# Expert weights by ranked expert: four fixed experts first, then a pattern of shared and full-width steps

## The reference, cut to what matters

```python
p_group = softmax(hf @ w_group + b_group)            # 4 groups
g_sel = argmax(p_group)
fine = (hf @ w_router + b_router).reshape(N, 4, 8)
top_v, top_i = lax.top_k(fine[g_sel], 2)             # two experts of the group
gate = softmax(top_v) * gate_g
expert = g_sel * 8 + top_i                           # 32 experts, 512 x 2 = 1024 routed rows
# for every expert e, on the rows routed to it:
gt, up = split(x_rows @ w_gu[e], 2)                  # 1024 -> 2 x 256
y = (silu(gt) * up) @ w_down[e]                      # 256 -> 1024
out[token] += gate * y
```

## Time and profile before

| | us |
|---|---|
| median of 3 runs | 2167.5 (2164.75 to 2168.77) |
| the profiled execution | 2168.4 |
| its span, first to last instruction | 2166.6 |
| first expert step starts (PE) | 1872.2 |
| last expert matmul ends | 2144.7 |
| PE busy | 2075.0 (96%) |
| bytes moved | 284.9 MB |

### The profile page before, as it was taken

One profiled execution on the slowest core, in us unless ns is written; L12 is line 12 of the kernel. 1 busy time (PEld: TensorE's weight loads), 2 busy tenths in 40 slices (PEclk: granted clock), 3 DMA queues, 4 the chain that ended last, 5 costly groups with the idle time before them and its releaser, 6 DMA issues.

```text
span 2166.6 us, 31540 instructions
## 1 busy us (share of the span) xinstructions
PE 2075.0 (96%) x13636; PEld 1524.9 (70%) x13636; DVE 1106.3 (51%) x1777; ACT 734.0 (34%) x1130; POOL 161.5 (7%) x140
## 2 busy tenths in 40 slices
PE   8999999999999998999999999999899999898887
PEld 6886688888888785788888887566788848532223
DVE  8886555335436876555335446476633353421114
ACT  6445632212324446532212333244322213311112
POOL 1220000000000320000000020000000001011121
PEclk9999999999999999999999999999999999899999
DMA  5222033322222231122222221312111315699996
GB/s 191 69 84 79 20 122 122 121 102 97 96 97 69 79 103 39 40 97 98 98 97 97 97 79 66 107 40 78 60 61 61 114 63 236 269 417 419 419 416 240
DMA packets 52254, 284.89 MB, mean 131 GB/s; under 512 B 9280, under 2 KB 9536, under 8 KB 22160
## 3 DMA queue, kind: packets, MB, share of 16 engines
q1 hardware_dynamic: 45344, 264.32, 32.9%
q0 software_dynamic: 6192, 17.64, 2.1%
q10 hardware_dynamic: 576, 0.87, 0.1%
HBM read 270.41 MB, written 22.02 MB: 135 GB/s over the span
## 4 chain that ended last, share of the span: by engine, by line
PE 75%; DMA 9%; DVE 9%; ACT 4%; issue 1%; SPq 1%; DVEq 0%; ACTq 0%
PE psum L126 73%; DMA ring_moe<-in_w_dn 8%; DVE A_mix L139 3%; PE psum L129 2%; ACT A_mix L133 1%; DVE WL L139 1%; DVE A_second L139 1%; ACT A_mix L136 1%; ACT WH L133 1%; SPq L171 1%; DMA M<-in_m 1%; DVE A_mix L165 1%; DVE A_second L147 0%; DVE A_mix L147 0%; DVE A_mix L159 0%
## 5 line engine op out<-in xcount | busy, mean ns | idle before, releaser
L139 DVE TENSOR_TENSOR WL<-raw,WH 128x1024 fp32r<-128x1024 f32 x236 | 300.8, 1277 | 351.3 <-ACT WH L133 350.8
L133 ACT ACTIVATE WH<-raw 128x1024 fp32r<-128x1024 f32 x236 | 247.5, 1054 | 356.9 <-PE psum L126 341.6
L126 PE MATMUL psum<-HH,WH 128*128 128x512 f32 x736 | 299.6, 407 | 17.6 <-DVE HL L147 10.0
L126 PE MATMUL psum<-R_op,WH 128*128 128x512 f32 x1024 | 316.1, 390 | 0.0
L126 PE MATMUL psum<-R_ffn,WH 128*128 128x512 f32 x1024 | 315.3, 389 | 0.0
L126 PE MATMUL psum<-HL,WH 128*128 128x512 f32 x736 | 288.5, 392 | 0.0
L126 PE MATMUL psum<-HH,WL 128*128 128x512 f32 x736 | 288.5, 392 | 0.0
L126 PEld LDWEIGHTS psum<-R_op,WH 128*128 128x128 f32 x1024 | 192.2, 188 | 40.6 <-issue 1.0
L126 PEld LDWEIGHTS psum<-R_ffn,WH 128*128 128x128 f32 x1024 | 192.2, 188 | 39.9
L126 PE MATMUL psum<-R_op,WL 128*128 128x512 f32 x512 | 199.3, 389 | 0.0
L126 PE MATMUL psum<-R_ffn,WL 128*128 128x512 f32 x512 | 199.3, 389 | 0.0
(11 more groups left out here) (205 smaller groups left out, 2494.9 us busy)
## 6 DMA issues: line engine op xcount, KB each, us to landing
ring_moe<-in_w_gu SPq DMA_DIRECT2D x45, 1024.0 KB, 28.6
raw<-in_w_in SPq DMA_DIRECT2D x41, 1024.0 KB, 5.0
raw<-in_w_up SPq DMA_DIRECT2D x32, 1024.0 KB, 5.0
raw<-in_w_down SPq DMA_DIRECT2D x32, 1024.0 KB, 4.9
ring_moe<-in_w_dn SPq DMA_DIRECT2D x23, 1024.0 KB, 28.5
raw<-in_w_out SPq DMA_DIRECT2D x12, 1024.0 KB, 4.9
X<-in_w_gu SPq DMA_DIRECT2D x10, 1024.0 KB, 27.5
raw<-in_w_gu SPq DMA_DIRECT2D x9, 1024.0 KB, 26.3
```

Source lines behind the costliest of these rows:

```text
L126: return self.raw.matmul(o, l, r, start=start, stop=stop)
L133: return self.raw.activation(o, i, f, scale=scale)
L139: return self.raw.tensor_tensor(o, a, b, op)
```

## The change

The 18 steps become 20, in the order of the letters in `STEPS`. S is one of the experts 0 to 3, alone on all 128 rows. The experts 4 to 31 are ranked by their counts on the chip: the four with the most rows are the D steps, alone on 128 rows; the other 24 share the twelve P steps, two by two with 64 rows each. There are no spill units; the loop behind the flag stays, in units of 128 rows. The ring has 16 slots (twelve in `RX`). SP loads the twelve chunks of the experts 0 to 3; the other 84 are gathered by POOL with the index `wix` that DVE makes from the ranking. The lists are split differently: `list` holds the four S steps, `list2` the 16 ranked ones. In each iteration p of its loop POOL issues the gather of the tokens of p+2, the scatter of p-1, then the weights. The order in which slots are used again is that in which they are spent (`spent`, `held`).

```diff
-NRING = 13
-NOWN = 9
-PAIRS = 18
-SPILL = 3
+NRING = 16
+NOWN = 12
+STEPS = "SSSSPPPDPPPDPPPDPPPD"
+NSTEP = len(STEPS)
...
+        def sides(p):
+            return (0, 1) if STEPS[p] == "P" else (0,)
...
+        spent = []
+        for p in range(NSTEP):
+            spent += ups(p) + (downs(p - 1) if p else [])
+        spent += downs(NSTEP - 1)
+        XW = [k for k in spent if STEPS[k[1]] == "S"] + [k for k in spent if STEPS[k[1]] != "S"]
+        XN = {key: n for n, key in enumerate(XW)}
+        place_of = list(range(3, 14)) + [2, 0, 1, 14, 15]
+        held = [None] * NRING
+        for n in range(NRING, len(XW)):
+            held.append(XN[spent[n - NRING]])
+            place_of.append(place_of[held[n]])
```

In `mo_pe`, `up` (and `down` likewise):

```diff
-                            t = e.mm(b[lo:lo + 64, :], mo.XT[p % 2][:, kt, lo:lo + 64], w[:, k * S:(k + 1) * S], kt == 0, kt == 7)
+                            t = e.mm(b[r, :], mo.XT[p % 2][:, kt, r], w[:, k * S:(k + 1) * S], kt == 0, kt == 7)
```

In `mo_pool`, with `sorted_in` in the place of `spilled`:

```diff
+            def sorted_in(n):
+                kind, p, side = XW[n][0:3]
+                i = 3 * (nth[p] if STEPS[p] == "D" else 4 + nth[p] + 12 * side) + (2 if kind == "dn" else XW[n][3])
+                if n >= NRING:
+                    e.wait_ge(*at(*let_go(held[n])))
+                e.gather(ring(n), dn_rows if kind == "dn" else gu_rows, mo.wix[:, i:i + 1]).then_inc(*sent(came(n), *XW[n]))
 
             gather(0)
             gather(1)
-            for p in range(PAIRS):
-                if p < PAIRS - 2:
+            e.wait_ge(*at("mo_dve", "wix"))
+            e.wait_ge(*at("mo_pe", "xr", 3, 1))
+            for n in range(12, NRING):
+                sorted_in(n)
+            for p in range(NSTEP):
+                if p < NSTEP - 2:
                     gather(p + 2)
                 if p == 1:
                     e.wait_ge(*at("zero", 15))
                 if p and p - 1 not in LATE:
                     scatter(p - 1)
                 for n in range(NRING, len(XW)):
-                    if XW[n][1] >= 32 and let_go(n - NRING)[1:3] in (("up", p), ("dn", p - 1)):
-                        spilled(n)
+                    if let_go(held[n])[1:3] in (("up", p), ("dn", p - 1)):
+                        sorted_in(n)
```

In `mo_dve`, the ranking; its last instruction counts `wix`:

```diff
+            e.tt(mo.gt, bcast(mo.key, 1, 28), bcast(mo.key[:, 4:32], 2, 32), ALU.is_gt).then_inc(*did("mo_dve", "gt"))
...
+            step(e.red(mo.pos[:, 4:32], mo.gt, ADD), "pos")
+            step(e.tt(mo.t, mo.oh, bcast(mo.pos, 1, 8), MUL), "q0")
+            step(e.red(mo.q, mo.t, ADD), "q")
...
+            step(e.tt(mo.eq, bcast(mo.pos[:, 4:32], 1, 28), bcast(c("io128")[:, 4:32], 2, 28), ALU.is_equal), "eq", 0)
+            step(e.tt(mo.eq, mo.eq, bcast(c("iota")[:, 4:32], 1, 28), MUL), "eq", 1)
+            step(e.red(mo.eid, mo.eq, ADD), "eq", 2)
...
+            t.then_inc(*did("mo_dve", "wix"))
```

In `sp_program`:

```diff
-            for n in range(NOWN):
+            for n in range(9):
                 sp_expert(e, n)
             e.wait_ge(*at("mo_pe", "lg", 3))
-            for n in range(NOWN, NOWN + 2):
+            for n in (9, 10):
                 sp_expert(e, n)
+            e.wait_ge(*at("mo_pe", "sum"))
+            sp_expert(e, 11)
...
-            e.wait_ge(*at("mo_pe", "xr", 3, 1))
-            for n in range(NOWN + 2, len(XW)):
-                if XW[n][1] < 32:
-                    sp_expert(e, n)
```

More of the change, by code:

```diff
@@ L2296, in build @@
         NB = 3
+        ar = Arena(A_moe, 0, NMOE)
+        mo.Xg, mo.Y = ([ar.take(D) for _ in range(NB)] for _ in range(2))
         mo.htok = t3(A_moe[:, 0:4 * D], 4)
[L2298 to L2301, removed]
+        mo.at_tok = [R_late[:, 2 * D + i * S:2 * D + (i + 1) * S] for i in range(2)]
@@ L2318, in build @@
[L2318 to L2323, removed]
+        mo.pm = t3(ar.take(128), 4)
+        work = ar.take(384)
@@ new lines, in build @@
+        mo.t, mo.Mk = t3(work[:, 0:256], 8), t3(work[:, 256:384], 4)
+        mo.t1, mo.t2 = mo.t[:, 0:4, :], mo.t[:, 4:8, :]
+        mo.RB = [work[:, i * 192:(i + 1) * 192].rearrange("p (k e r) -> p k e r", k=4, r=3) for i in range(2)]
+        mo.RA = [ar.take(48).rearrange("p (k e r) -> p k e r", k=4, r=3) for _ in range(2)]
+        mo.root = ar.take(4)
+        mo.r12, mo.row, mo.big, mo.q, mo.hi, mo.sid = (ar.take(8) for _ in range(6))
+        mo.cnt, mo.key, mo.base, mo.pos, mo.cap, mo.ne, mo.uc, mo.ux, mo.uw, mo.tw = (ar.take(32) for _ in range(10))
@@ L2363, in build @@
[L2363 to L2367, removed]
+        vacant = [ring(XN[k]) for k in spent[len(spent) - NRING:] if place_of[XN[k]] > 4]
+        Y2N = [XN[k] for k in spent[len(spent) - NRING:] if place_of[XN[k]] > 4][0:4]
+        mo.Y2 = vacant[0:4]
@@ new lines, in mo_dve @@
+            step(e.ts(mo.big, mo.r12, 63.5, BIG, ALU.is_gt, MUL), "hi")
+            e.tt(mo.big, mo.big, mo.sid, MUL)
+            step(e.stt(mo.row, mo.hi, 64.0, mo.r12, MUL, ADD), "row0")
+            e.tt(mo.row, mo.row, mo.big, ADD)
+            step(e.stt(mo.sid, mo.hi, -12.0, mo.q, MUL, ADD), "sid")
+            step(e.tt(mo.S, bcast(c("io128")[:, 4:20], 1, 8), bcast(mo.sid, 2, 16), ALU.is_equal), "S")
+            for i, (own, g) in enumerate((("tok2", mo.g1), ("tok3", mo.g2))):
+                one = mo.S[:, 4 * i:4 * i + 4, :]
+                e.tt(mo.RB[i][:, :, :, 0], one, bcast(c("tok4"), 2, 16), MUL)
+                e.tt(mo.RB[i][:, :, :, 1], one, bcast(c(own), 2, 16), MUL)
+                e.tt(mo.RB[i][:, :, :, 2], one, b4(g, 16), MUL)
+                e.tt(t3(mo.PB[i], 4), bcast(c("io128"), 1, 4), bcast(mo.row[:, 4 * i:4 * i + 4], 2, 128), ALU.is_equal).then_inc(
+                    *did("mo_dve", "PB", i))
@@ L2916, in step @@
                     e.wait_ge(*last("ov_dve"))
[L2918 to L2919 removed]
+                for j in range(UNITS):
+                    if j:
                         e.wait_ge(*at("ov_y", j - 1))
@@ L2999, in ov_act @@
                 e = inner(e0)
-                for j in range(SPILL, UNITS):
+                for j in range(UNITS):
                     e.wait_ge(*at("ov_pe", j, "gu"))
```

277 lines of the change are left out of this document (120 added, 157 removed).

## The result

The changed kernel takes 2176.05 us (median of 7 runs, 2173.42 to 2177.9), the kernel before 2168.29 us beside it: a ratio of 1.0038, interval 1.0027 to 1.0049. It moves 9.6 MB less and is 8 us slower. The forecast was no change, 2167 us.

A forecast was written before the change was run, and what follows sets the result against it. The prediction took four steps as bound by PE, twelve by DMA, then a PE tail. Its terms ended the last matmul at 2143.9 against 2144.7, so 2167.5 - 0.8 gave 2166.7, rounded to 2167 us; range 2157 to 2184.

The forecast's parts named there:

- The sum: Last stage: step 4's end, load issue, latency, queued DMA and PE's remaining work end the matmuls at 2143.9, 0.8 us earlier.
- The start: First four full-width steps: begin 0.3 us later than before, 11.9 us each, step 4 ending at 1931.7.
- From here DMA is never out of work: From the first load after step 4: 16.3 us of DMA work per two-expert iteration, against 10.4 of POOL.
- Rival A: One-expert steps: POOL's queue runs dry, PE waits for tokens, 6 to 15 us lost, 2173 to 2182; chance 0.35.
- The sign named for rival A: In 1940:2120, a GB/s row under 410 would show the queue running dry.
- The tail: PE's work after the tokens of step 19 land: 20.4 us, with 1.0 for the turn and 3.6 for step 17's down.
- the loads of the step before are queued too: Argument against the queue running dry at one-expert steps: earlier loads would still be in POOL's queue.
- The rate: POOL's filled queue carrying all ranked weights: 417 GB/s, 2.50 us a chunk; the other end was 346 GB/s.
- Rival B: Expert stage: DMA keeps up and PE bounds it; in full 2138, the likely part 2157 to 2163; chance 0.23.
- C: Spill loop: a slot overflows and the loop of 15 units runs, costing over 110 us; chance 0.01.
- PE waits on tokens and never on weights: Sign of being right: PE waits on token gathers, not weights, in steps 7, 8, 11, 12, 15 and 16.
- The gain on offer: Weight loads of the stage: 96 chunks instead of 105, nine fewer, 22.5 us of DMA.

The follow-up runs named there:

- both changes of order: Against the changed kernel, POOL gathers tokens three steps ahead instead of two and issues loads before the scatter: 2152.31 us, 0.9931 of the kernel before.

## Why the prediction was wrong

The sum, term by term:

| term | predicted | measured |
|---|---|---|
| first expert step | 1872.5 | 1873.48 |
| step 4 begins | 1919.7 | 1919.26 |
| scatter 3, first load | 1932.9, 1934.2 | 1932.26, 1933.58 |
| from that load to the tokens of step 19 | 2.7 + 186.6 = 189.3 | 197.5 |
| PE behind them | 20.4 | 23.1 |
| last expert matmul ends | 2143.9 | 2154.2 |
| the rest | 21.9 | 21.9 |

- **The start was right.** The four full-width steps, the scatter behind step 4 and the first load came within 0.7 us. POOL's first four loads went out from 1872.36 on, inside the 1866 to 1874 given for `wix`, and 15 ranked chunks were issued before step 4 ended, as counted. The first step was 1.0 us later than forecast, made good by full-width steps of 11.4 to 11.6 instead of 11.9 us. A single execution can't tell whether the ranking causes that 1.0: the start moves by up to 8 us between executions.
- **The step that failed is "From here DMA is never out of work".** It compared supply and use over a whole iteration (16.3 us of work, 10.4 of POOL) and not the moments. The loop has an order: tokens land, PE works, POOL issues, data flows. Rival A looked at this loop and gave it 2 us of margin, 8.0 against 10.0 us. But its 8.0 ended at the issue of the load; the 2.7 us of latency, which the sum itself uses, were left out. 10.7 against 10.0 is a gap already. Measured behind the tokens at 2044.55, with the lower clock behind the wait (1.45 and 4.97 us instead of 1.0 and 3.6), it is 11.8. The missing shares in the windows of 5 us (1935:1940, 1990:1995, 2050:2060, 2110:2120) add up to 5.9 us of the 8.2; the rest is spread over windows whose share stands a little under 1.02, and no run here separates its cause. The amount to move was right: 194.8 us at 398 GB/s (1936.28 to 2131.05, a share of 0.98) are 77.5 MB, and 186.6 us at 419 GB/s are 78.2. The sign named for rival A, a GB/s row under 410, came four times (348, 409, 388, 394).
- **The tail was mis-sized by the clock**, 2.7 us in all: the turn took 1.97 instead of 1.0 and the down matmuls of step 17 5.80 instead of 3.6 us, and the rest was 0.5 us shorter. Rival A named the lower clock for the waits in the loop; the sum used full-clock rows for the same kind of wait at its end.
- **Rival A was what happened**: its mechanism, its place (behind the one-expert steps) and its time (2173 to 2182). That the measured time lies in the stated range of 2157 to 2184 is due to this rival alone and not to the sum. It got 0.35, beside 0.41 for no change; the argument "the loads of the step before are queued too" stood against it. The DMA view refutes that: at its issue a chunk was, by the median, about the fourth in the queue.
- **The rate was right.** A filled queue of POOL ran at 418 to 420 GB/s (both changes of order, 1940 to 2080), where the sum took 417 from one stretch of 5 us. The Trainium skill gives 341 GB/s for a 1 MB transfer ("DMA: Bandwidth & Descriptors", section "Measured (HBM→SBUF, 128 partitions, SWDGE, issued from GpSimd)"). That does not hold for chunks that queue up: these 418 to 420 GB/s are chunks of 1 MiB.
- **Rivals B and C did not come.** B's time, 2157 to 2163, was reached only once the order was changed (tokens three ahead, 2158.58). POOL has 219 instructions in the page after, so no loop over spilled rows ran.
- **PE waits on tokens and never on weights**, right, but not how often: the waits were 27.4 us in ten, in the steps named (7, 8, 11, 12, 15, 16) and in 9, 13, 17 and 19 besides.
- **"The gain on offer", 22.5 us, was real as a bound and not reached.** With the order put right 15 us come in (0.9931): 18 by the stages, less what is given back behind them. PE bounds the stage up to 2020, where it is busy for all 20 us of each window from 1880 on; from 2020 to 2100 it idles 2.6 to 2.9 us in three windows of four, beside DMA at 408 to 418 GB/s, so there both count. Rival B had PE's steps end at 2115 for a start at 1872.5, 242 us; the stage is 254.

## What to carry to other kernels

When a small transfer that an engine waits for moves into a queue with large ones, it lands behind all that was issued before it: issue it a step earlier, or keep it in a queue of its own. When a queue is fed by what an engine lets go, compare the time from landing to the next data, latency included and at the clock that follows a wait, with the work that lies behind the awaited transfer; the depth of the ring is not in that comparison. Put the issues that wait for the end of a step (the scatter here) behind those that could go during it. In these runs the filled queue had a price at the end: the last scatter took 7 us more to land.

## What the runs showed of the hardware

- One indirect DMA of POOL per 1 MiB chunk, each taking POOL 1.0 us and 0.3 us to the next, kept DMA at 418 to 420 GB/s for 140 us (both changes of order, 1940 to 2080), tokens and scatters included.
- A wait of 2.26 us was followed by matmuls at a granted clock of 0.57 in 2089:2093 (the lower level is 1.2 GHz, 0.50) and 1.00 again in 2094:2096, though the turn right behind the wait was still quick (1.09 us). PE's timeline in the kernel after, with two matmuls of the same kind 3.6 us apart:

```profile
2088.29 1.09 PE L129 MATMUL psum<-C,A_moe 128*128 128x128 f32 x8 [2.26 <-DMA A_moe<-h_rows,A_moe]
...
2090.02 1.06 PE L126 MATMUL psum<-raw,RS 128*64 128x512 f32 x1
...
2093.64 0.59 PE L126 MATMUL psum<-raw,RS 128*64 128x512 f32 x1
```

  After 1.75 us of waiting (1984.59) the down matmuls took their 3.60 us. The price of a wait is thus more than its length, and it can come a little later.
- A chunk lands 11.9 us after its issue in one order and 30.4 in another, with the faster kernel on the side of 30.4: a long time from issue to landing means a filled queue here, not a slow one.
- A filled queue doesn't end at once. With both changes of order the last chunk was issued at 2083.69, and the DMA share, a mean of 16 engines, fell from 1.02 in 2093:2095 over 0.75 in 2103:2105 to 0.10 in 2117:2119; in the kernel after, whose last chunk was issued at 2123.37, it fell from 0.98 in 2129:2131 to 0.07 in 2133:2135. Which engines lag, and why, no run here shows.
